# The last layer's down product as rows, with the activations stationary, in a two-layer hybrid decoder

## The chip, the cores and the metric

The kernel runs on one core of a Trainium2 chip. The metric is the device time in microseconds of one execution. Five engines work side by side: TensorE (PE, with its weight loads shown apart as PEld), VectorE (DVE), ScalarE (ACT), GpSimd (POOL) and SyncE (SP, which issues most DMAs).

## The reference

256 tokens with 2048 features go through two layers, each a token mixer and a dense SwiGLU feed-forward network (FFN), and a last RMS norm. All is float32. Layer 0 mixes by a convolution module, layer 1 by gated linear attention.

```python
D_MODEL = 2048; SEQ = 256; D_FF = 5632
def rms_norm(x, g):
    return x * lax.rsqrt(jnp.mean(x * x, axis=-1, keepdims=True) + EPS) * g

def swiglu_ffn(h, w_gate_up, w_down):
    a, g = jnp.split(h @ w_gate_up, 2, axis=-1)
    return (jax.nn.silu(a) * g) @ w_down

for i in range(DEPTH):
    h = mixer_i(rms_norm(x, norm_mix_g[i]))
    x = x + h
    x = x + swiglu_ffn(rms_norm(x, norm_ffn_g[i]), ffn_w_gate_up[i], ffn_w_down[i])
return rms_norm(x, final_norm_g)
```

## The kernel before

**Layout.** The residual stream lies in SBUF as `res`, features on the 128 partitions and the 256 tokens along the row: 16 tiles of 128 features, `res[:, 4g:4g+4, :]` being group g of 512 features. Products stay nearly float32 by a split: each operand is a high part (a rounded copy, made by ACT) and a low part (the remainder, by DVE), and hi\*hi + hi\*lo + lo\*hi are summed in PSUM.

**Weights.** SP streams all matrices in chunks of 1 MB (512 input features by 512 output features, as four k-tiles `kt`) through a ring of four buffers `raw`. For each chunk ACT writes `w_hi` (L496), DVE writes `w_lo` (L785), PE multiplies and signals `w_used`. SP loads a chunk once the remainder of the chunk four places before is made; ACT turns a chunk to `w_hi` once PE is done with the chunk four places before. All engines run in program order, so the order of the code is the order of the work.

**The wide form.** For all products but two, PE holds weights stationary (128 by 128) and moves activations. `wide_chunk` issues for each of 4 k-tiles and 4 output tiles a pair: 512 moving columns against `w_hi` (tokens of the high part and of the low part together, L1291), 256 against `w_lo` (L1293). That is 32 matmuls and 32 weight loads a chunk. The halves land in different columns of a bank, so DVE adds two tensors to the residual per group, `from_hi` (L1006) and `from_lo` (L1014).

**The FFN** runs in three parts (`PARTS`) of 4, 4 and 3 pairs: each pair makes 512 hidden features (8 gate/up chunks), then the part's hidden features go through `w_down`: 4 output groups of 4 (or 3) chunks, added to `res`. A group uses four of the eight PSUM banks (slot s = g % 2), and PE may start group g once DVE has read group g - 2 (`acc_read`).

**The row form.** The attention values (L1623) and the last output group of the last layer (`half_chunk`, L1685) are made the other way: activations stationary (128 tokens), 512 weight columns moving, so the result has tokens on partitions. A chunk is, for each token half a, 4 k-tiles by 3 matmuls of 512 columns (hi\*hi, hi\*lo, lo\*hi): 24 matmuls and 24 weight loads.

**The end.** In the last part of layer 1, ACT squares each finished group (L530) and multiplies it by the gain (L535), DVE reduces the squares over the features (L804 to L810). While PE makes the last group as rows, it turns `res` of that group into PSUM (`half_residual`, L1676), transposes the other three groups (`output_rows`, L1670) and sums the squares over partitions (L1701). When a token half is done (`half_out`), ACT squares the last group with a sum (L766), takes the root (L770), DVE inverts it, both scale the four groups of rows into `out_rows` (L775, L1247, L1250), and SP stores two pieces of 512 KB. The second half's tail ends the kernel.

## Time and profile before

| | |
|---|---|
| timed runs | 2193.17, 2194.74, 2196.64 us; median 2194.74 us |
| span of the profiled execution | 2192.3 us, first to last instruction |
| PE / PEld busy | 2177.5 us (99%) / 1922.3 us (88%) |
| DVE busy | 1405.7 us (64%) |
| ACT busy | 991.0 us (45%) |
| DMA | 400.46 MB, mean 183 GB/s |

The profile is one execution, whose own time is its span of 2192.3 us; the median of the timed runs is 2.4 us longer, for what lies around the span and for the spread of the runs. PE's busy time overlaps with itself, since matmuls are pipelined: what a matmul costs is read from start to start, not from its duration. A "wait" in these views is the idle time of an engine before an instruction, put down to what came last.

### The profile page before, as it was taken

How to read it: one execution, taken by the hardware profiler on the slowest of the kernel's cores; microseconds unless marked ns; L12 is line 12 of the kernel's file. 1: busy time of each engine (PE TensorE's matmuls, PEld its weight loads, DVE VectorE, ACT ScalarE, POOL GpSimd, SP SyncE). 2: the span in 40 equal slices, each digit the busy share in tenths (PEclk: the TensorE clock that was granted, in tenths of full speed). 3: DMA queues.
4: the chain of work that ended last, by engine and by line, in shares of the span. 5: the costliest groups of instructions: out<-in, count | busy, mean ns of one | idle time of the engine just before them, and what ended most of it. 6: DMA issues, size and time to landing. Idle time of an engine off the chain costs nothing.

```text
span 2192.3 us, 32460 instructions
## 1 busy us (share of the span) xinstructions
PE 2177.5 (99%) x12992; PEld 1922.3 (88%) x12992; DVE 1405.7 (64%) x1314; ACT 991.0 (45%) x821; POOL 203.2 (9%) x107
## 2 busy tenths in 40 slices
PE   8999999999999999999999999999999999999998
PEld 8999888888888888888888888888888888888887
DVE  7999785555555655556667777675555555555655
ACT  6666554443344433444363444554443344433444
POOL 7998000000000000000000000000000000000000
PEclk9999999999999999999999999999999999999999
DMA  9664456555555555655544435655555555555552
GB/s 248 182 186 158 152 191 214 188 195 191 187 175 198 174 205 179 210 173 192 192 154 154 150 120 192 209 175 199 185 191 192 189 194 179 198 188 187 174 209 77
DMA packets 250043, 400.46 MB, mean 183 GB/s; under 512 B 6407, under 2 KB 72143, under 8 KB 249935
## 3 DMA queue, kind: packets, MB, share of 16 engines
q1 hardware_dynamic: 249406, 398.74, 54.7%
q8 instruction: 57, 0.93, 0.2%
q0 software_dynamic: 352, 0.56, 0.1%
q14 instruction: 20, 0.16, 0.0%
q10 hardware_dynamic: 208, 0.07, 0.0%
HBM read 397.24 MB, written 2.10 MB: 182 GB/s over the span
## 4 chain that ended last, share of the span: by engine, by line
PE 92%; DVE 4%; issue 2%; DVEq 1%; DMA 0%; ACT 0%; SPq 0%; ACTq 0%
PE bank L1291 55%; PE bank L1293 27%; PE bank L1623 4%; DVE bank L942 2%; PE bank L1378 1%; PE bank L1608 1%; PE bank L1685 1%; PE bank L1365 1%; DMA raw<-in_conv_w_in 0%; DVEq L920 0%; PE bank L1393 0%; PE bank L1368 0%; DVE bank L936 0%; DVE bank L923 0%; PE bank L1397 0%
## 5 line engine op out<-in xcount | busy, mean ns | idle before, releaser
L1291 PE MATMUL bank<-x_both,w_hi 128*128 128x512 f32 x3328 | 1156.7, 394 | 0.0
L785 DVE TENSOR_TENSOR w_lo<-raw,w_hi 128x2048 fp32r<-128x2048 f32 x343 | 779.2, 2290 | 527.1 <-ACT w_hi L496 526.9
L496 ACT ACTIVATE w_hi<-raw 128x2048 fp32r<-128x2048 f32 x374 | 707.4, 1909 | 627.7 <-PE bank L1293 599.2
L1293 PE MATMUL bank<-x_both,w_lo 128*128 128x256 f32 x3328 | 922.6, 277 | 0.0
L1291 PEld LDWEIGHTS bank<-x_both,w_hi 128*128 128x128 f32 x3328 | 624.8, 188 | 145.8 <-issue 0.8
L1291 PE MATMUL bank<-h_both,w_hi 128*128 128x512 f32 x1872 | 649.4, 394 | 0.4 <-DVE h_both L986 0.4
L1293 PEld LDWEIGHTS bank<-x_both,w_lo 128*128 128x128 f32 x3328 | 625.5, 188 | 0.1
L1293 PE MATMUL bank<-h_both,w_lo 128*128 128x256 f32 x1872 | 518.5, 277 | 0.0
L1291 PEld LDWEIGHTS bank<-h_both,w_hi 128*128 128x128 f32 x1872 | 351.0, 187 | 82.0 <-issue 0.5
L1293 PEld LDWEIGHTS bank<-h_both,w_lo 128*128 128x128 f32 x1872 | 351.4, 188 | 0.0
L1378 PE MATMUL bank<-x_both,w_hi 128*128 128x256 f32 x832 | 150.0, 283 | 0.0
L376 POOL TENSOR_TENSOR w_lo<-raw,w_hi 128x2048 fp32r<-128x2048 f32 x31 | 143.5, 4633 | 5.6 <-DVE w_lo L785 5.6
L942 DVE SCALAR_TENSOR_TENSOR bank<-u,dw,bank 128x256 f32<-128x256 f32 x334 | 137.9, 485 | 0.0
L1378 PEld LDWEIGHTS bank<-x_both,w_hi 128*128 128x128 f32 x832 | 129.8, 192 | 0.1
L1378 PE MATMUL bank<-x_both,w_lo 128*128 128x256 f32 x416 | 117.7, 283 | 0.0
L485 POOL DMA_DIRECT2D last_gain<-in_final_norm_g x1 | 0.6, 597 | 1115.3 <-PE bank L1293 1115.3
L1623 PE MATMUL bank<-w_hi,x_both 128*128 128x512 f32 x256 | 81.2, 393 | 0.0
L1378 PEld LDWEIGHTS bank<-x_both,w_lo 128*128 128x128 f32 x416 | 79.9, 192 | 0.0
L476 POOL DMA_DIRECT2D gate_w<-in_gla_gate_w x1 | 1.2, 1226 | 631.2 <-PE bank L1293 631.2
L1054 DVE TENSOR_TENSOR tmp<-bank,act 128x1024 f32<-128x1024 f32 x22 | 27.0, 1225 | 49.6 <-ACT act L660 49.6
L665 ACT ACTIVATE act<-bank 128x1024 f32<-128x1024 f32 x22 | 22.6, 1027 | 79.7 <-PE bank L1293 79.7
L660 ACT ACTIVATE act<-bank 128x1024 f32<-128x1024 f32 x22 | 22.6, 1027 | 77.0 <-PE bank L1293 77.0
(227 smaller groups left out, 1232.2 us busy)
## 6 DMA issues: line engine op xcount, KB each, us to landing
raw<-in_ffn_w_gate_up SPq DMA_DIRECT2D x176, 1024.0 KB, 5.1
raw<-in_ffn_w_down SPq DMA_DIRECT2D x88, 1024.0 KB, 5.1
raw<-in_gla_w_in SPq DMA_DIRECT2D x48, 1024.0 KB, 5.3
raw<-in_conv_w_in SPq DMA_DIRECT2D x32, 1024.0 KB, 6.0
raw<-in_conv_w_out SPq DMA_DIRECT2D x16, 1024.0 KB, 5.1
raw<-in_gla_w_out SPq DMA_DIRECT2D x16, 1024.0 KB, 6.9
x_rows<-in_x SPq DMA_DIRECT2D x4, 512.0 KB, 6.4
out<-out_rows SPq DMA_DIRECT2D x4, 512.0 KB, 3.1
```

The source lines that it names most:

```text
L376: nc.gpsimd.tensor_tensor(w_lo[k][:, :, :], raw[k][:, :, :], w_hi[k][:, :, :].bitcast(F32), ALU.subtract).then_inc(lo_done, 1)
L496: nc.scalar.activation(w_hi[k][:, :, :], raw[k][:, :, :], ACT.Copy).then_inc(hi_done, 1)
L660: nc.scalar.activation(part_lo[0], from_lo[0], ACT.Copy).then_inc(lo_kept[0], 1)
L665: nc.scalar.activation(part_lo[1], from_lo[1], ACT.Copy).then_inc(lo_kept[1], 1)
L785: nc.vector.tensor_tensor(w_lo[k][:, :, :], raw[k][:, :, :], w_hi[k][:, :, :].bitcast(F32), ALU.subtract).then_inc(lo_done, 1)
L942: nc.vector.scalar_tensor_tensor(out=to, in0=tap, scalar=w, in1=acc, op0=ALU.mult, op1=ALU.add).then_inc(tap_done, 1)
L1054: nc.vector.tensor_tensor(tmp[0][:, :, :], from_hi[0], part_lo[0], ALU.add).then_inc(acc_read[0], 1)
L1291: mm(to, w_hi[k][:, kt, cols], xx[:, :, k0 + kt, :], start=(first and kt == 0), stop=False, skip_group_check=True)
L1293: ins = mm(to[:, 0:T], w_lo[k][:, kt, cols], xx[:, 0, k0 + kt, :], start=False, stop=(last and kt == 3), skip_group_check=True)
L1365: mm(to, conv_view(w_hi[k])[:, kt, :], xx[:, kt, :], start=(kt == 0 and j == 0), stop=False)
L1378: ins = mm(slot[t][:, 2 - 2 * h, :], conv_view(w[k])[:, kt, :], xx[:, kt, :], start=(kt == 0 and j == 0), stop=(kt == KT - 1 and j == 2))
L1623: ins = mm(rows_[:, a, :], xx[:, 4 * j + kt, tok], w[j][:, kt, :], start=(j == 0 and kt == 0 and i == 0), stop=(j == 3 and kt == 3 and i = ...
```

## The change

The whole down product of layer 1 is made in the row form, in all three parts and all four groups. For that the residual has to be rows too: in the first part PE transposes it, 8 transposes of 128 by 128 a group (`res_bank`, the two spare banks of the slot), before the group's products, and ACT copies it back in place (`res_rows`). DVE then adds one tensor a group (`row_group`). In the last part ACT squares each group with a sum along the row (`row_squares`), DVE multiplies by the gain (`gain_rows`), and no transposes, no reductions over features and no sums by PE are left in the last group: PE adds the residual of the last group by one product with the identity per token half. The loads of the gain over all partitions grow from 256 KB to 1 MB. The final scaling works in place in `out_rows`. The loops over groups of the first two parts are written out.

The core of the diff (semaphores and removed counterparts are cut):

```diff
-        last_gain = sb("last_gain", [P, GW], 32 * K)
-        last_scratch = sb("last_scratch", [P, GW], 34 * K)
+        last_gain = sb("last_gain", [P, D], 32 * K)
+        last_scratch = sb("last_scratch", [P, 4, GW], 40 * K)
...
+        rows_bank = [bank[:, 4 * s:4 * s + 2, :] for s in range(2)]
+        res_bank = [bank[:, 4 * s + 2:4 * s + 4, :] for s in range(2)]
+        res_rows = [res[:, 4 * g:4 * g + 4, :].rearrange("p (a k) t -> p a (k t)", a=2) for g in range(4)]
...
             pool.wait_ge(w_used, C_END - 12)
-            pool.dma_start(last_gain[:, :], final_norm_g.rearrange("(a d) -> a d", a=1)[:, 3 * GW:].broadcast_to([P, GW])
+            pool.dma_start(last_gain[:, :], final_norm_g.rearrange("(a d) -> a d", a=1).broadcast_to([P, D])
...
+            def row_squares(use0, g):
+
+                scalar.wait_ge(acc_read[g % 2], (use0 + g) // 2 + 1)
+                for a in range(2):
+                    ins = nc.scalar.activation(squared_rows[g][:, a, :], res_rows[g][:, a, :], ACT.Square,
+                                               accum_out=sq_part[:, 3 * a + g:3 * a + g + 1])
+                ins.then_inc(rows_sq, 1)
...
+                    if l == 1 and pt == 0:
+                        for g in range(4):
+                            hi_group(d0 + 4 * g, 2)
+                            scalar.wait_ge(res_t, g + 1)
+                            nc.scalar.activation(res_rows[g], res_bank[g % 2], ACT.Copy).then_inc(res_turned, 1)
+                            hi_group(d0 + 4 * g + 2, 2)
...
-                for g in range(2):
-                    scalar.wait_ge(half_rows[a], g + 1)
-                    nc.scalar.activation(out_rows[:, a, g * GW:(g + 1) * GW], rows_bank[a][g], ACT.Copy,
-                                         scale=rstd_tok[:, a:a + 1]).then_inc(rows_act[a], 1)
+                nc.scalar.activation(out_rows[:, a, 0:2 * GW], out_rows[:, a, 0:2 * GW], ACT.Copy,
+                                     scale=rstd_tok[:, a:a + 1]).then_inc(rows_act[a], 1)
...
+            def row_group(c_end, g, first):
+
+                dve.wait_ge(w_used, c_end + 1)
+                if first:
+                    dve.wait_ge(res_turned, g + 1)
+                nc.vector.tensor_tensor(res_rows[g], rows_bank[g % 2], res_rows[g], ALU.add).then_inc(acc_read[g % 2], 1)
...
+            def rows_and_gains(c0, chunks, use0):
+
+                for g in range(3):
+                    lo_group(c0 + chunks * g, chunks)
+                    row_group(c0 + chunks * (g + 1) - 1, g, False)
+                    if g == 1:
+                        dve.wait_ge(gain_in, 16)
+                    if g >= 1:
+                        gain_rows(use0, g - 1)
+                gain_rows(use0, 2)
...
+            def row_chunk(c, g, j, a, chunks, started=False):
+
+                k, tok = c % RING, slice(a * P, (a + 1) * P)
+                for kt in range(4):
+                    for n, (hh, w) in enumerate(((h_hi, w_hi), (h_hi, w_lo), (h_lo, w_hi))):
+                        ins = mm(rows_bank[g % 2][:, a, :], hh[:, 4 * j + kt, tok], w[k][:, kt, :],
+                                 start=(not started and j == 0 and kt == 0 and n == 0),
+                                 stop=(j == chunks - 1 and kt == 3 and n == 2), skip_group_check=True)
+                return ins
+
+            def rows_product(c0, u0, h0, chunks, first):
+
+                for g in range(4 if chunks == RING else 3):
+                    free_slot(g % 2, (u0 + g) // 2)
+                    if first:
+                        for a in range(2):
+                            for b in range(4):
+                                ins = nc.tensor.transpose(res_bank[g % 2][:, a, b * P:(b + 1) * P],
+                                                          res[:, 4 * g + b, a * P:(a + 1) * P], ident[:, :])
+                        ins.then_inc(res_t, 1)
+                    for j in range(chunks):
...
-            half_residual(0)
-            half_chunk(0, 0)
-            output_rows(0, 0)
...
             for a in range(2):
...
+                mm(rows_bank[1][:, a, :], ident[:, :], res_rows[3][:, a, :], start=True, stop=False, skip_group_check=True)
+                for j in range(3):
+                    c = C_END - 3 + j
+                    pe.wait_ge(lo_done, c + 1)
+                    ins = row_chunk(c, 3, j, a, 3, started=True)
+                ins.then_inc(half_out, 1)
```

PE, before, where the first part's gate/up chunks end and its first down chunk begins (names: `h_both` the hidden features, `w_hi`, `w_lo` the weights; the moving operand stands first):

```order
L1501 UNCONDITIONAL_BRANCH
L1501 ISA
L1302 ISA [waits acc_read0]
L1291 MATMUL bank<-h_both,w_hi_57 128x512 [waits hid_ready,lo_done]
L1293 MATMUL bank<-h_both,w_lo_61 128x256
L1291 MATMUL bank<-h_both,w_hi_57 128x512
L1293 MATMUL bank<-h_both,w_lo_61 128x256
```

PE, of the change, at the same place:

```order
L1583 MATMUL bank<-ident,res 128x128 [waits acc_read0]
L1583 MATMUL bank<-ident,res 128x128 x7
L1571 MATMUL bank<-w_hi_57,h_both 128x512 [waits hid_ready,lo_done]
L1571 MATMUL bank<-w_lo_61,h_both 128x512
L1571 MATMUL bank<-w_hi_57,h_both 128x512 x2
L1571 MATMUL bank<-w_lo_61,h_both 128x512
```

Eight transposes now stand ahead of the products of each of the first part's four groups, pairs of 512 and 256 columns have become triples of 512, and the waits are the same ones.

PE, before, around the last output group's first chunk:

```order
L1676 MATMUL bank<-ident,res 128x128 [waits acc_read1]
L1676 MATMUL bank<-ident,res 128x128 x3
L1685 MATMUL bank<-w_hi_58,h_both 128x512 [waits lo_done]
L1685 MATMUL bank<-w_lo_62,h_both 128x512
...
L1670 MATMUL bank<-ident,act 128x128 [waits xn_done]
L1670 MATMUL bank<-ident,act 128x128 x3
L1685 MATMUL bank<-w_hi_59,h_both 128x512 [waits lo_done]
```

PE, of the change, at the same place:

```order
L1756 MATMUL bank<-res,ident 128x512 [waits acc_read1]
L1571 MATMUL bank<-w_hi_58,h_both 128x512 [waits lo_done]
L1571 MATMUL bank<-w_lo_62,h_both 128x512
...
L1571 MATMUL bank<-w_hi_58,h_both 128x512
L1571 MATMUL bank<-w_hi_59,h_both 128x512 [waits lo_done]
```

The products of the last group now follow one another with no transposes between them; the six blocks of four transposes (L1670) and the sums (L1701) are gone, and one matmul of 512 columns a token half takes the place of four of 128.

DVE, of the change, in the last part, from the second group's last remainder on:

```order
L1044 TENSOR_TENSOR res<-bank,res 128x1024 [waits w_used]
L1050 TENSOR_TENSOR out_rows<-res,last_gain 128x2x512 [waits acc_read0,gain_in]
L808 TENSOR_TENSOR w_lo_62<-raw_54,w_hi_58 128x2048 [waits hi_done]
L808 TENSOR_TENSOR w_lo_63<-raw_55,w_hi_59 128x2048 [waits hi_done]
L808 TENSOR_TENSOR w_lo_64<-raw_56,w_hi_60 128x2048 [waits hi_done]
```

The wait for the gain (`gain_in`) stood at the end of the program before, behind the last remainders; now it stands ahead of the last three.

## Rows read from the trace of the kernel before

**Rows 1.** The page: span, busy time, and PE's busy share and granted clock in slices
```profile
span 2192.3 us, 32460 instructions
PE 2177.5 (99%) x12992; PEld 1922.3 (88%) x12992; DVE 1405.7 (64%) x1314; ACT 991.0 (45%) x821; POOL 203.2 (9%) x107
PEclk9999999999999999999999999999999999999999
```

**Rows 2.** The page: shares of the chain that ended last
```profile
PE 92%; DVE 4%; issue 2%; DVEq 1%; DMA 0%; ACT 0%; SPq 0%; ACTq 0%
```

**Rows 3.** Waits of ACT from 2100 to 2170 us: total, times, longest
```profile
ACT w_hi L496 <- PE bank L1293: 14.0, 5, 3.6
```

**Rows 4.** Timeline of ACT, layer 1: start us, duration us, in brackets the idle time before
```profile
1910.31 1.92 ACT L496 ACTIVATE w_hi<-raw 128x2048 fp32r<-128x2048 f32 x1 [3.63 <-PE bank L1293]
...
1971.33 1.92 ACT L496 ACTIVATE w_hi<-raw 128x2048 fp32r<-128x2048 f32 x1 [3.63 <-PE bank L1293]
```

**Rows 5.** Timeline of ACT, attention values, one whole row chunk without other PE work
```profile
1237.96 1.93 ACT L496 ACTIVATE w_hi<-raw 128x2048 fp32r<-128x2048 f32 x1 [1.25 <-PE bank L1623]
1243.40 1.91 ACT L496 ACTIVATE w_hi<-raw 128x2048 fp32r<-128x2048 f32 x1 [3.51 <-PE bank L1623]
```

**Rows 6.** Timeline of PE, last output group
```profile
2169.56 0.40 PE L1685 MATMUL bank<-w_lo,h_both 128*128 128x512 f32 x1
...
2171.87 0.39 PE L1685 MATMUL bank<-w_hi,h_both 128*128 128x512 f32 x1
...
2176.99 0.48 PE L1685 MATMUL bank<-w_hi,h_both 128*128 128x512 f32 x1
2177.31 0.39 PE L1685 MATMUL bank<-w_lo,h_both 128*128 128x512 f32 x1
...
2185.04 0.39 PE L1685 MATMUL bank<-w_hi,h_both 128*128 128x512 f32 x1
```

**Rows 7.** Timeline of PE, start of the kernel: eight transposes and what follows
```profile
10.58 1.04 PE L1329 MATMUL bank<-ident,x_rows 128*128 128x128 f32 x8
11.45 0.28 PE L1319 MATMUL bank<-ident 128*128 128x128 f32 x1
```

**Rows 8.** The chain that ended last, from 2165 us: start us, us, what
```profile
2165.42 0.89 PE bank L1676 x8
2166.31 2.74 PE bank L1685 x12
2169.05 0.44 PE bank L1670 x4
...
2176.24 1.00 PE bank L1676 x8
2177.24 8.21 PE bank L1685 x36
```

**Rows 9.** Timeline: last gate/up chunk's copy, one remainder, one group squared
```profile
2115.54 1.03 ACT L665 ACTIVATE act<-bank 128x1024 f32<-128x1024 f32 x1 [3.63 <-PE bank L1293]
...
2145.28 2.29 DVE L785 TENSOR_TENSOR w_lo<-raw,w_hi 128x2048 fp32r<-128x2048 f32 x1 [1.60 <-ACT w_hi L496]
...
2151.34 1.06 ACT L530 ACTIVATE tmp<-res 128x1024 f32<-128x1024 f32 x1 [6.09 <-DVE res L1014]
```

**Rows 10.** Timeline, the end: ACT's and DVE's last work, SP's last issues
```profile
2186.72 1.27 ACT L775 ACTIVATE out_rows<-bank,rstd_tok 128x512 f32<-128x512 f32 x2 [0.23 <-DVE rstd_tok L1245]
...
2187.38 0.74 DVE L1250 TENSOR_SCALAR out_rows<-bank,rstd_tok 128x512 f32<-128x512 f32 x1
2188.01 0.81 SPq L366 DMA_DIRECT2D out<-out_rows  x2
```

**Rows 11.** Windows 1090.66 to 1094.00 and 2165.26 to 2176.10: engines' busy time, then PEclk, DMA share, GB/s
```profile
1090.66:1094.00 3.34, 3.34 (x11) 2.86 (x11) 3.34 (x8) 0.00 (x0) 0.00 (x0) 0.50 0.38 81
2165.26:2176.10 10.84, 10.84 (x63) 9.19 (x61) 7.29 (x6) 3.26 (x7) 0.00 (x0) 1.00 0.01 2
```

**Rows 12.** DMA issues from 2105 us on: KB each, median us to landing
```profile
last_gain<-in_final_norm_g POOLq DMA_DIRECT2D x1, 256.0 KB, 4.3
```

More of the change, by code:

```diff
@@ L260, in trunk @@
         half_out = sem("half_out")
-        half_rows = [sem(f"half_rows{a}") for a in range(2)]
+        res_t = sem("res_t")
+        res_turned = sem("res_turned")
+        rows_sq = sem("rows_sq")
+        rows_gain = sem("rows_gain")
+        rows_total = sem("rows_total")
         half_sq = sem("half_sq_done")
-        bias_stat = sem("bias_stat")
         bias_done = sem("bias_done")
@@ L363, in _ @@
                 for n, rows in enumerate((rows_act, rows_vec)):
-                    sp.wait_ge(rows[a], 2)
+                    sp.wait_ge(rows[a], n + 1)
                     cols = slice(2 * n * GW, (2 * n + 2) * GW)
@@ L681, in ffn @@
                             gain(g)
-                            if l == 0 and g == 0:
+                            if g == 0:
                                 scalar.wait_ge(gate_in, 48)
@@ L1014, in residual_group, with gain_rows @@
                 nc.vector.tensor_tensor(to, from_lo[s], to, ALU.add).then_inc(acc_read[s], 1)
+            def row_group(c_end, g, first):
[3 more added lines that the diff above has]
+                nc.vector.tensor_tensor(res_rows[g], rows_bank[g % 2], res_rows[g], ALU.add).then_inc(acc_read[g % 2], 1)
+            def gain_rows(use0, g):
+                dve.wait_ge(acc_read[g % 2], (use0 + g) // 2 + 1)
+                cols = slice(g * GW, (g + 1) * GW)
+                nc.vector.tensor_tensor(out_rows[:, :, cols], res_rows[g], over(last_gain[:, cols], 2),
+                                        ALU.mult).then_inc(rows_gain, 1)
+            def rows_and_gains(c0, chunks, use0):
+                for g in range(3):
+                    lo_group(c0 + chunks * g, chunks)
[5 more added lines that the diff above has]
+                gain_rows(use0, 2)
             def residual_and_squares(c0, n_group, n0, gains, chunks=4):
@@ L1075, in ffn @@
                     d0 = c0 + 8 * pairs
-                    if pt < 2:
+                    if l == 1 and pt < 2:
+                        for g in range(4):
+                            lo_group(d0 + 4 * g)
+                            row_group(d0 + 4 * g + 3, g, pt == 0)
+                    elif l == 1:
+                        rows_and_gains(d0, pairs, u0 + 2 * pairs)
+                    elif pt < 2:
                         with dve.Fori(0, 2) as i:
@@ L1664, in _ @@
             ffn(1, 4 * KT, 16, 8)
-            def output_rows(g, a):
-                pe.wait_ge(xn_done, 2 * KT + 4 * g + 4)
-                for b in range(4):
-                    ins = nc.tensor.transpose(rows_bank[a][g][:, b * P:(b + 1) * P], act[:, 4 * g + b, a * P:(a + 1) * P],
-                                              ident[:, :])
-                ins.then_inc(half_rows[a], 1)
-            def half_residual(a):
-                for b in range(4):
-                    mm(rows_bank[a][3][:, b * P:(b + 1) * P], res[:, 12 + b, a * P:(a + 1) * P], ident[:, :],
-                       start=(b == 0), stop=False, skip_group_check=True)
@@ L1679, in half_chunk @@
-            def half_chunk(a, j):
-                c = C_END - 3 + j
-                pe.wait_ge(lo_done, c + 1)
-                k, tok = c % RING, slice(a * P, (a + 1) * P)
-                for kt in range(4):
-                    for n, (hh, w) in enumerate(((h_hi, w_hi), (h_hi, w_lo), (h_lo, w_hi))):
-                        ins = mm(rows_bank[a][3], hh[:, 4 * j + kt, tok], w[k][:, kt, :], start=False,
-                                 stop=(j == 2 and kt == 3 and n == 2), skip_group_check=True)
-                if j == 2:
-                    ins.then_inc(half_out, 1)
```

59 lines of the change are left out of this document (30 added, 29 removed).

## The prediction

> **What bounds the kernel now.** I read the page first: PE is busy 99% of a span of 2192.3 us, at the full clock in every slice [rows 1]. The chain that ended last is PE for 92% [rows 2]. Then the waits in the stage that changes: ACT, which prepares the weights, idles up to 3.6 us at a time until PE has freed a buffer [rows 3]. So ACT, DVE (behind ACT) and the DMAs (behind DVE) are ahead of PE, and PE is ahead of nobody: a microsecond more or less on PE in this stage is a microsecond of the kernel, and one on another engine is nothing so long as it stays under these 3.6 us a chunk. Only behind PE's last product do ACT, DVE and the stores set the end.
>
> **What a chunk costs, before.** PE's rows overlap, so I take the pace from ACT, which starts on a new buffer each time PE ends a chunk: 12 starts from 1910.31 to 1971.33 us, so 11 chunks of the wide form in 61.02 us, **5.547 us a chunk** [rows 4]. This stretch lies in the second part's down product.
>
> **What a chunk costs as rows.** The kernel has this form in two places. In the last group, from 2177.31 to 2185.04 us, 34 steps of one matmul take 7.73 us: 0.2274 us each, 5.457 us for 24 [rows 6]. Among the attention values one chunk with nothing between takes 5.44 us [rows 5]. The dearest stretch is 2169.56 to 2171.87 us, 10 steps in 2.31 us, so 0.2310 us and 5.544 us a chunk [rows 6]; DVE and ACT are at work there, in the first half of the group. Columns do not explain a gain: both forms move 12,288 columns a chunk. The difference is 24 matmuls in place of 32. Moving 512 columns at 2.4 GHz is 0.2133 us, so 0.014 us comes on top of each matmul; a wide pair is 5.547/16 = 0.3467 us against 0.3200 us of columns, 0.0133 us a matmul again. Eight fewer are 0.107 us. I take the 5.457 us of the longest stretch, a saving of 0.092 us a chunk, since this stretch has company from ACT or DVE for a part of it only, as a chunk has.
>
> The Trainium skill (TensorE: Matmul & The Clock Gate, Back-to-back issue gap) gives an isolated matmul its columns at the clock plus 2.5 ns. By that rule eight matmuls fewer are 0.02 us, the 41 chunks give 0.8 us, and the sum would come out near 2195.4 us, no gain. The trace disagrees, with its 13 ns a matmul in a stream that has a weight load ahead of each [rows 4, 6].
>
> **The terms.**
> 1. Chunks that change form: 4 groups of 4 chunks in each of two parts, 3 groups of 3 in the last, 41. 41 x 0.092 = **3.8 us less**. Ends: 41 x 0.107 = 4.4 (a chunk of 5.44) and 41 x 0.003 = 0.1 (the dearest stretch).
> 2. Transposes of the residual, 8 in each of 4 groups, on PE, where nothing hides them. Eight in a row at the start of the kernel take 11.45 - 10.58 = 0.87 us [rows 7]. In the last group four cost 0.44 us of the chain [rows 8], and that holds a slower first step of the product behind them: 2176.99 to 2177.31 is 0.32 us against 0.23, 0.09 more [rows 6]. So eight are between 2 x 0.44 - 0.09 = 0.79 and 0.87 + 0.09 = 0.96 us. I take 0.88, **3.5 us more**; ends 3.2 and 3.8. Below nothing is excluded: PE is busy before and behind, and the instructions are added.
> 3. The last group. Before, PE's chain from 2165.42 to 2185.45 us is 20.03 us [rows 8]. It holds two residual products (0.89 and 1.00), 72 matmuls of rows, three blocks of transposes at 0.44, and the sums. What is left is residual plus 36 matmuls, twice: 2 x (0.89 + 8.21) = 18.2 us, **1.8 us less**. The residual product's 512 columns are now one matmul, not four of 128; I give it the price of the four, since the columns are the same. Ends: 0.79 to 1.00 for it and 8.16 to 8.32 for the rows, so 2.1 and 1.4.
> 4. Behind the last product, square, root and inverse are the same. ACT's scaling was two copies of 512 from PSUM, 1.27 us [rows 10], and becomes one of 1024 in SBUF; the nearest row is 1.06 us [rows 9]. SP issues both last stores at 2188.01, right behind ACT [rows 10], so **0.2 us less**. DVE's last product (0.74 us) now reads SBUF, not PSUM; the rows have no such form at this size. If it were twice as fast, the second store could follow sooner: 0.5 us at best, 0 at worst. The 12 transposes that stood behind the last product ran beside ACT and cost nothing before.
>
> Costed at nothing: ACT's four copies of the turned residual, about 1.06 us each by the same size [rows 9], in the 3.6 us that it idles in every chunk [rows 3, 4]. They stand behind the wait `res_t`, and the next `w_hi` is queued behind them, for which DVE and then PE wait; but ACT comes to it after a `w_hi` that itself waits for the group's first chunk, so the transposes have long been done. Without that cover it would be 4 us. DVE does one add a group in place of two, and one gain product in place of a reduction and an add: less work. The squares by rows come where ACT's squares and gains stood, and the gains leave ACT. The bias needs DVE's add, ACT's squares and three small operations behind the third group, and is asked for half a group later, 0.89 + 8.21 = 9.1 us [rows 8].
>
> Sum: -3.8 + 3.5 - 1.8 - 0.2 = -2.3 us, against the profiled span 2192.3 - 2.3 = 2190.0 us. The median of the timed runs is 2.4 us above that span, so 2194.7 - 2.3 = **2192.4 us**. This is 0.11%; a measurement of this kernel tells about 0.2%, or 4.4 us, from no change. The best ends together: -4.4 + 3.2 - 2.1 - 0.5 = -3.8, 2190.9 us. The worst: -0.1 + 3.8 - 1.4 = +2.3, 2197.0 us.
>
> **The rivals.**
> - *The row form is no cheaper.* With ACT and DVE at work beside it, as in most of each chunk, rows go at the 5.54 us of the dearest stretch. Then -0.1 + 3.5 - 1.8 - 0.2 = +1.4, **2196.1 us**. For it: that stretch is the one with most work beside it. Against it: the chunk of 5.44 us among the attention values has a whole `w_hi` beside it as well [rows 5]. The Trainium skill's rule above comes out between this and the forecast, and speaks for it.
> - *The clock falls behind the transposes*, and the kernel is **slower**. At 1090.66 us the granted clock is 0.50, the 1.2 GHz level, for 3.3 us [rows 11], after a block of small products of the attention gate. In these 3.34 us PE starts 11 matmuls, some 5.3 pairs, which take 5.3 x 0.347 = 1.8 us at 2.4 GHz, so a fall costs 1.5 us. Behind each of the four blocks of transposes it would be 6 us: 2192.4 + 6.0 = **2198.4 us**; it decides from two falls on (3 us against the 2.3 won). Against it: the last group has three blocks of four transposes, the sums and a residual product within 10.8 us at clock 1.00 [rows 11]. The Trainium skill (TensorE: Matmul & The Clock Gate, Part 4: PE-mode transpose) states that the full clock does not engage for transposes; the rows here show none that lost it.
> - *The gain comes late*, slower too. It grows from 256 KB in 4.3 us [rows 12] to 1 MB, 17 us in proportion, and its wait now stands ahead of the last three remainders on DVE. It is issued when the last gate/up chunk ends, at 2115.5 us [rows 9]; PE needs the first of those remainders at 2165.4 [rows 8], and one takes 2.3 us [rows 9]. DVE can wait until 2163, 47 us after the issue. Past that each microsecond is one of the kernel. It would need three times the proportional time.
> - *Clearly faster*: best ends for all terms and something more, such as transposes half hidden behind the weight loads. Under 2190.3 us.
>
> **How the numbers follow.** Forecast (2190.9 to 2194.5) 0.58; rows no cheaper (2194.5 to 2197.0) 0.18; the clock 0.07, half of it over 4.4 us slower; the gain or another new wait 0.04, slower; clearly faster 0.13. So faster by over 0.2%: 0.13, with 0.02 of the forecast that spread between runs carries over, 0.15; slower by over 0.2%: 0.035 + 0.04, with a little of the rest 0.09; within it 0.76. The range takes in both sums of ends: low 2190.3, a little under the best, high 2197.0.
>
> **What would show it.** In the profile of after: ACT's starts on `w_hi` in the down stages 5.44 to 5.47 us apart (5.54: the first rival). PE's matmuls fewer by 41 x 8 = 328 before what the rest adds. From a group's first transpose to its first row matmul 0.8 us, and the next step 0.3. From the last group's first instruction to `half_out` 18.2 us. PEclk 1.00 in the first down stage; DVE not idle for `last_gain`. The prediction is wrong if PE idles anywhere in the written-out groups, or if the chunk pace is outside 5.44 to 5.54 us.

## The result: the change is 3.35 us slower, 0.16%

| | median of the runs, us | lowest to highest | runs |
|---|---|---|---|
| before | 2195.54 | 2193.0 to 2197.6 | 18 |
| with the change | 2198.89 | 2196.42 to 2202.1 | 18 |

The ratio is 1.0016, with a 95% interval of 1.001 to 1.0022. The forecast was 2192.4 us, range 2190.3 to 2197.0: it has the wrong sign and misses by 6.5 us, of which 0.8 us is the median of before, which came out higher over 18 runs than over the first 3.

The page of the change: span, busy time and PE's granted clock, which answer to [rows 1]. PE's share of the chain that ended last is 92% as before.

```profile
span 2197.6 us, 31653 instructions
PE 2182.4 (99%) x12656; PEld 1918.8 (87%) x12656; DVE 1388.6 (63%) x1302; ACT 991.1 (45%) x820; POOL 203.1 (9%) x107
PEclk9999999999999999999999999999999999999999
```

PE makes 336 matmuls fewer and is busy 5 us longer, at the same clock. So no other engine became the bound: something on PE got dearer. The place is found by laying the same program point of both kernels side by side: the start of the ACT instruction that PE's last matmul of a chunk releases.

| program point | before, us | change, us | change is behind by |
|---|---|---|---|
| first w_hi behind the convolution's mixing | 228.43 | 229.52 | 1.09 |
| layer 0's FFN, first copy (L660, now L674) | 334.19 | 337.20 | 3.01 |
| a query/key copy (L693, now L717) | 1098.11 | 1100.01 | 1.90 |
| layer 1's FFN, part one's gate/up ends | 1627.43 | 1629.35 | 1.92 |
| part one's down product ends | 1716.18 | 1720.09 | 3.91 |
| part two's gate/up ends | 1893.67 | 1900.98 | 7.31 |
| part two's down product ends | 1982.42 | 1988.09 | 5.67 |
| part three's gate/up ends | 2115.54 | 2123.76 | 8.22 |
| PE's last product ends | 2185.47 | 2190.84 | 5.37 |

(1982.42 is the last start of [rows 4] plus two chunks.) Up to 1627 us the two kernels run the same instructions on PE, and their difference there comes and goes: more on it below. From there on the change loses 1.99, 3.40 and 2.55 us and wins 1.64 and 2.85. The down products do what was forecast. The two losses of 3.40 and 2.55 us, 5.95 us together, are in the **gate/up products of parts two and three, which the change doesn't touch**.

Timeline of ACT in the change, from the last row chunks of part one into part two's gate/up (start us, duration us, in brackets the idle time before):

```profile
1714.71 1.92 ACT L502 ACTIVATE w_hi<-raw 128x2048 fp32r<-128x2048 f32 x1 [3.52 <-PE bank L1571]
1720.09 1.92 ACT L502 ACTIVATE w_hi<-raw 128x2048 fp32r<-128x2048 f32 x1 [3.46 <-PE bank L1571]
1725.73 1.93 ACT L502 ACTIVATE w_hi<-raw 128x2048 fp32r<-128x2048 f32 x1 [3.72 <-PE bank L1349]
1731.38 1.92 ACT L502 ACTIVATE w_hi<-raw 128x2048 fp32r<-128x2048 f32 x1 [3.72 <-PE bank L1349]
...
1742.69 1.03 ACT L674 ACTIVATE act<-bank 128x1024 f32<-128x1024 f32 x1 [3.73 <-PE bank L1349]
```

The same chunks before:

```profile
1721.73 1.92 ACT L496 ACTIVATE w_hi<-raw 128x2048 fp32r<-128x2048 f32 x1 [3.63 <-PE bank L1293]
1727.27 1.92 ACT L496 ACTIVATE w_hi<-raw 128x2048 fp32r<-128x2048 f32 x1 [3.63 <-PE bank L1293]
...
1738.37 1.03 ACT L660 ACTIVATE act<-bank 128x1024 f32<-128x1024 f32 x1 [3.63 <-PE bank L1293]
```

A wide chunk takes 5.65 us behind the row form where it takes 5.55 us before, the same 32 matmuls, with ACT waiting for PE in both (3.73 and 3.63 us: the wait shows the pace). It goes on for all 32 and 24 chunks: (7.31 - 3.91) / 32 = 0.106 us each. PE starts nothing late and doesn't idle; each pair is longer. Timeline of PE in the change, three pairs (they start 0.36 and 0.35 us apart, 0.353 over the whole chunk of 16):

```profile
1721.64 0.40 PE L1347 MATMUL bank<-x_both,w_hi 128*128 128x512 f32 x1
1721.88 0.28 PE L1349 MATMUL bank<-x_both,w_lo 128*128 128x256 f32 x1
1722.00 0.40 PE L1347 MATMUL bank<-x_both,w_hi 128*128 128x512 f32 x1
1722.24 0.28 PE L1349 MATMUL bank<-x_both,w_lo 128*128 128x256 f32 x1
1722.35 0.40 PE L1347 MATMUL bank<-x_both,w_hi 128*128 128x512 f32 x1
```

and before (0.35 and 0.35 us apart, 0.3467 over the chunk [rows 4]):

```profile
1721.87 0.40 PE L1291 MATMUL bank<-x_both,w_hi 128*128 128x512 f32 x1
1722.10 0.28 PE L1293 MATMUL bank<-x_both,w_lo 128*128 128x256 f32 x1
1722.22 0.39 PE L1291 MATMUL bank<-x_both,w_hi 128*128 128x512 f32 x1
...
1722.57 0.40 PE L1291 MATMUL bank<-x_both,w_hi 128*128 128x512 f32 x1
```

It isn't the clock. Windows of the change: the first down part with its transposes, and the gate/up of part two (us, busy time and count by engine, then PEclk, DMA share, GB/s; PEclk is the last figure but two):

```profile
1623.50:1720.00 96.50, 96.50 (x451) 80.53 (x450) 47.35 (x24) 38.08 (x23) 0.00 (x0) 1.00 0.55 186
1720.00:1901.00 181.00, 181.00 (x1026) 156.90 (x1025) 99.29 (x54) 74.44 (x47) 0.00 (x0) 1.00 0.55 186
```

### The profile page after: what moved, and what is told of

Read it like the earlier page. It is cut to its first block, busy times and chain, and to the rows that moved or that the text cites. A ratio compares the mean times of both kernels' runs of the same rounds, so it can differ in the third digit from the quotient of the medians.

```text
span 2197.6 us, 31653 instructions
## 1 busy us (share of the span) xinstructions
PE 2182.4 (99%) x12656; PEld 1918.8 (87%) x12656; DVE 1388.6 (63%) x1302; ACT 991.1 (45%) x820; POOL 203.1 (9%) x107
## 4 chain that ended last, share of the span: by engine, by line
PE 92%; DVE 4%; issue 2%; DVEq 1%; DMA 0%; ACT 0%; SPq 0%; ACTq 0%
PE bank L1347 48%; PE bank L1349 24%; PE bank L1571 11%; PE bank L1710 4%; DVE bank L965 2%; PE bank L1434 1%; PE bank L1695 1%; PE bank L1421 1%; DVEq L943 0%; PE bank L1449 0%; PE bank L1424 0%; DMA x_rows<-in_x 0%; DVE bank L959 0%; PE bank L1453 0%; DVE bank L946 0%
## 5 line engine op out<-in xcount | busy, mean ns | idle before, releaser
L1347 PE MATMUL bank<-h_both,w_hi 128*128 128x512 f32 x1216 | 423.6, 393 | 0.4 <-DVE h_both L1009 0.4
L1349 PE MATMUL bank<-h_both,w_lo 128*128 128x256 f32 x1216 | 340.0, 280 | 0.0
L1347 PEld LDWEIGHTS bank<-h_both,w_hi 128*128 128x128 f32 x1216 | 227.8, 187 | 52.4 <-issue 0.5
L1349 PEld LDWEIGHTS bank<-h_both,w_lo 128*128 128x128 f32 x1216 | 229.7, 189 | 0.0
L1571 PE MATMUL bank<-w_hi,h_both 128*128 128x512 f32 x704 | 219.5, 391 | 0.0
L1571 PEld LDWEIGHTS bank<-w_hi,h_both 128*128 128x128 f32 x704 | 132.2, 188 | 27.8 <-issue 0.5
L1571 PE MATMUL bank<-w_lo,h_both 128*128 128x512 f32 x352 | 137.0, 389 | 0.0
L1571 PEld LDWEIGHTS bank<-w_lo,h_both 128*128 128x128 f32 x352 | 66.1, 188 | 14.0 <-issue 0.5
```

Of the source, the lines that this page charges most:

```text
L1347: mm(to, w_hi[k][:, kt, cols], xx[:, :, k0 + kt, :], start=(first and kt == 0), stop=False, skip_group_check=True)
L1349: ins = mm(to[:, 0:T], w_lo[k][:, kt, cols], xx[:, 0, k0 + kt, :], start=False, stop=(last and kt == 3), skip_group_check=True)
L1571: ins = mm(rows_bank[g % 2][:, a, :], hh[:, 4 * j + kt, tok], w[k][:, kt, :], start=(not started and j == 0 and kt == 0 and n == 0), stop= ...
```

## The experiments

The two theories at the start: **(A)** the wide form has two paces, and PE keeps through a stretch the one in which it entered it; entered from rows that is the longer. **(B)** the place of the code, or something else that the change moved, makes these loops longer.

### Is it there without the change, and every time?

Both kernels again, unchanged.

> The kernel before, unchanged, profiled once more. In its first profile all wide stages went at 5.55 us a chunk; in the first profile of the change the output product of the convolution (228 to 331 us), of the same code in both, went at 5.65. If the pace is drawn anew in each execution (theory A: two paces, set by how a stage is entered), this profile may show 5.65 in some wide stage. If the pace is fixed by where the code lies (theory B), it shows 5.55 everywhere, as the first did.

> The change, unchanged, profiled once more. Theory A: the gate/up products behind the rows of the first two parts again at 5.65 us a chunk, since they are entered in the same way each time, while the stages at 228 us and 1064 us may differ from the first profile. Theory B: every stage exactly as in the first profile, those at 228 and 1064 us at 5.65 too.

The change took 2201.85 us, its gate/up chunks in parts two and three 5.65 us again. The kernel before took 2197.53 us, with all chunks of the last layer's FFN at 5.55 us. But in this execution of it the long pace stood elsewhere, in the convolution's output product and in both stretches of query/key chunks. For the first of these places, timeline of ACT, the kernel before run again, then its first profile:

```profile
228.61 1.92 ACT L496 ACTIVATE w_hi<-raw 128x2048 fp32r<-128x2048 f32 x1 [3.67 <-PE bank L1293]
...
256.88 1.91 ACT L496 ACTIVATE w_hi<-raw 128x2048 fp32r<-128x2048 f32 x1 [1.64 <-PE bank L1293]
```

```profile
228.43 1.92 ACT L496 ACTIVATE w_hi<-raw 128x2048 fp32r<-128x2048 f32 x1 [3.57 <-PE bank L1293]
...
256.16 1.92 ACT L496 ACTIVATE w_hi<-raw 128x2048 fp32r<-128x2048 f32 x1 [1.09 <-PE bank L1293]
```

And the first stretch of query/key chunks, the kernel before run again:

```profile
1078.41 1.91 ACT L496 ACTIVATE w_hi<-raw 128x2048 fp32r<-128x2048 f32 x1 [2.89 <-PE bank L1293]
1084.06 1.92 ACT L496 ACTIVATE w_hi<-raw 128x2048 fp32r<-128x2048 f32 x1 [3.73 <-PE bank L1293]
```

Five chunks lie between the two starts in the convolution: 28.27 us in the one and 27.73 us in the other, 5.65 and 5.55 each again, in one and the same program. The long pace isn't a thing of the change, then, and theory B as it was put (the first profile again, stage by stage) fails here already. This explains most of the differences ahead of 1627 us in the table too: the change's profile had the long pace in that stage (+1.92 us of the 3.01). One such stage is a good part of the 4.6 us between the shortest and the longest run of before.

### Break the stream behind the rows, or ahead of them

A product of one column with the identity (plain float32; PE shows two instructions for it) goes between the row blocks of parts one and two and the next gate/up loop. As the control, the same products stand ahead of the row blocks: same number, nearly the same places in the code.

```diff
+                    if l == 1 and pt > 0:          # behind the rows
+                        free_slot(0, u0 // 2)
+                        mm(bank[:, 0, 0:1], ident[:, :], ident[:, 0:1], start=True, stop=True, skip_group_check=True)
```

```diff
+                    if g == 0 and chunks == RING:  # control: ahead of the rows
+                        mm(bank[:, 0, 0:1], ident[:, :], ident[:, 0:1], start=True, stop=True, skip_group_check=True)
```

> The change with one float32 product of one column (two matmul instructions) behind the rows of parts one and two, ahead of the gate/up loop. Theory A (the slow pace comes from running straight from rows into the wide form): gate/up of parts two and three back to 5.55 us a chunk, 56 x 0.107 = 6.0 us less and 0.3 us more for the two products, so some 5.7 us under the change: 2193.2 us, under the kernel before by 2. Theory B (place of the code): the loop moves by two instructions only, and the time stays within 1 us of the change, or moves in both this run and the next.

> The control: the same two products at the other end of the row blocks, ahead of them, so that the code behind is moved by just as much, but the gate/up loop is entered from rows as in the change. Theory A: gate/up stays at 5.65 us a chunk, 2199 us. Theory B: the same time as the run with the product behind the rows.

| | us | ratio to before (2195.66) | gate/up chunk |
|---|---|---|---|
| product behind the rows | 2193.85 | 0.9992 (0.9983 to 1.0001) | 5.55 |
| product ahead of the rows | 2198.39 | 1.0016 (1.0006 to 1.0025) | 5.65 |

Timeline of ACT with the product behind the rows:

```profile
1719.09 1.92 ACT L502 ACTIVATE w_hi<-raw 128x2048 fp32r<-128x2048 f32 x1 [3.46 <-PE bank L1571]
1724.86 1.92 ACT L502 ACTIVATE w_hi<-raw 128x2048 fp32r<-128x2048 f32 x1 [3.86 <-PE bank L1349]
1730.41 1.92 ACT L502 ACTIVATE w_hi<-raw 128x2048 fp32r<-128x2048 f32 x1 [3.63 <-PE bank L1349]
```

One chunk of 5.77 us pays for the product, and the rest go at 5.55. Two products of one column take 4.5 us off the kernel against their twins ahead of the rows. Theory A stands so far, and the place of the code falls as the cause.

### What kind of product breaks it

Three other products at the same place behind the rows: 128 and 512 columns of the rounded type (fp32r) that the kernel's own products have, and, later, 128 columns of float32.

```diff
+                        mm(bank[:, 0, 0:P], h_hi[:, 0, 0:P], h_hi[:, 0, 0:P], start=True, stop=True, skip_group_check=True)  # short
```
```diff
+                        mm(bank[:, 0, :], h_hi[:, 0, 0:P], h_hi[:, 0:2, :], start=True, stop=True, skip_group_check=True)  # row
```
```diff
+                        mm(bank[:, 0, 0:P], ident[:, :], ident[:, :], start=True, stop=True, skip_group_check=True)  # float32
```

> As the run with the small product behind the rows, but the product is of the split type, 128 columns against 128 (one matmul instruction, no float32). If what matters is that a short instruction breaks the even beat of the rows, gate/up goes at 5.55 us a chunk. If it takes a float32 product, it stays at 5.65. The rhythm theory says 5.55, without much certainty.

> Control for any product at that place: one of the split type with 512 columns, which goes on in the beat of the rows. The rhythm theory: gate/up stays at 5.65 us a chunk. If any added product helps, whatever its length, 5.55.

> The change with a float32 product of 128 columns behind the rows (one column restored the fast pace, a split product of 128 columns did not). 5.55 in gate/up if it takes a float32 product; 5.65 if it takes a very short one.

One run of each: 2197.2, 2198.74 and 2191.54 us. With either fp32r product the chunks stay at 5.65 us, against my expectation for the short one; with the float32 product they are 5.55. The start that tells them apart, ACT with 128 columns of fp32r and then of float32:

```profile
1729.14 1.92 ACT L502 ACTIVATE w_hi<-raw 128x2048 fp32r<-128x2048 f32 x1 [3.73 <-PE bank L1349]
1734.80 1.92 ACT L502 ACTIVATE w_hi<-raw 128x2048 fp32r<-128x2048 f32 x1 [3.74 <-PE bank L1349]
```
```profile
1728.90 1.92 ACT L502 ACTIVATE w_hi<-raw 128x2048 fp32r<-128x2048 f32 x1 [3.63 <-PE bank L1349]
1734.45 1.92 ACT L502 ACTIVATE w_hi<-raw 128x2048 fp32r<-128x2048 f32 x1 [3.63 <-PE bank L1349]
```

So not any interruption does it, and with float32 1 and 128 columns both do. Of the products tried here only the plain float32 ones work. What in them does it isn't told apart: a float32 product is two matmuls and two weight loads in PE's trace, each fp32r product was one, and two fp32r products in a row were not tried.

### Does such a product always give the short pace?

The products behind the rows, with two more in the convolution's output product and one each ahead of query/key groups 2 and 3; the last four alone in the kernel before; and one small product ahead of the gate/up loops in the kernel before, where no rows stand. (The first of the two in the convolution adds a column of zeros to a bank in use.)

```diff
+                    if j == 2 and s == 0:
+                        pe.wait_ge(zero_set, 1)
+                        mm(bank[:, 0, 0:1], ident[:, :], zero[:, :], start=False, stop=False, skip_group_check=True)
...
+                if s == 0:
+                    mm(bank[:, 0, 0:1], ident[:, :], ident[:, 0:1], start=True, stop=True, skip_group_check=True)
...
+                if g in (1, 2):
+                    mm(bank[:, 4 * (g % 2), 0:1], ident[:, :], ident[:, 0:1], start=True, stop=True, skip_group_check=True)
```

> The change with the small products behind the rows, and four more: in the middle and in the second half of the convolution's output product (228 to 331 us), and ahead of the second and the third query/key group (1070 to 1142 us), the places where profiles of all kernels have shown now 5.55 and now 5.65 us a chunk. Theory: those stages at 5.55 in every run, some 1.0 us less on average at the first place and 0.7 at the second, 0.8 more for four products, so 2193 us and a narrower spread. Rival (the pace there is not set by the entry): 2194.6 us and the spread as before.

> The kernel before with the same four products in the convolution's output and the query/key groups, and no rows. By the theory 2194.8 us against 2195.7; then the run with all products against this one is the worth of the row form by itself, which the terms of the prediction put at 2.3 us less.

> The kernel before, all wide, with the small float32 product ahead of the gate/up loops of parts two and three of the last layer. In the runs with products at the query/key groups, the product stood behind a wide matmul of 256 columns and the stage went to 5.65 us a chunk. If the pace is set by how the beat is entered, and has nothing to do with rows as such, gate/up and down of part two (48 chunks) go at 5.65 here: 5 us slower, 2200 to 2201 us, and up to 8.7 us if the second product leaves it slow. If it is the rows that slow what follows, this kernel is 0.4 us slower than before, no more.

| | us | ratio to before |
|---|---|---|
| change, all products | 2194.31 | 0.9996 (0.9987 to 1.0005) |
| before, the four products | 2196.27 | 1.0004 (0.9995 to 1.0013) |
| before, a product ahead of gate/up | 2195.53 | 1.0002 (0.9992 to 1.0011) |

No. The first two came out 1.3 and 1.5 us over what was expected, and the runs spread as widely as before. Gate/up was at 5.55 us where rows stood ahead, and stayed at 5.55 us in the kernel before, where I had expected the product to bring the long pace. But both stretches of query/key groups were at the long pace behind their product, in both kernels (4 of 4). Timeline of ACT, the change with all products:

```profile
1077.14 1.92 ACT L505 ACTIVATE w_hi<-raw 128x2048 fp32r<-128x2048 f32 x1 [3.10 <-PE bank L1352]
1082.79 1.92 ACT L505 ACTIVATE w_hi<-raw 128x2048 fp32r<-128x2048 f32 x1 [3.73 <-PE bank L1352]
```

In the 13 other profiles with paired chunks, where no product stands there, the first of these stretches was long in 4 and the second in 8, the kernel before among both kinds. So a float32 product is no switch to the short pace. That it brings the long one here is likely from 4 of 4, and not shown. The two kernels with the four products differ by the change and its products behind the rows alone: 2196.27 - 2194.31 = 2.0 us in favour of the row form, with intervals (each about 2 us to either side) that overlap.

### Other ways out: order in a pair, the convolution's stage, rows in the last part only

```diff
+                        if lo_first:   # gate/up of parts two and three: 256 columns first
+                            mm(to[:, 0:T], w_lo[k][:, kt, cols], xx[:, 0, k0 + kt, :], start=(first and kt == 0), stop=False,
+                               skip_group_check=True)
+                            ins = mm(to, w_hi[k][:, kt, cols], xx[:, :, k0 + kt, :], start=False,
+                                     stop=(last and kt == 3), skip_group_check=True)
+                            continue
```

> The change, with the pairs of the gate/up loops of parts two and three in the other order: 256 columns against the low part first, then 512 against the high part. No product is added. If the entry sets the beat, the stage may fall into the fast one (5.55, some 6 us less than the change: 2193 us) or stay; it costs nothing. If the slow pace belongs to the code behind the rows, 2199 us.

It took 2198.71 us, ratio 1.0018 (1.0009 to 1.0028), with chunks of 5.65 us: turning the pair round changes nothing that these runs can tell.

The next has the products behind the rows and the two in the convolution's output product (the first two pieces of the diff of the section before).

> The products behind the rows, and the two in the convolution's output product, without those at the query/key groups that made things slower. 0.45 us more for the two, 1.0 less on average for the stage at 228 us: 2193.3 us, against 2193.85 with the products behind the rows alone, and no run over 2195.

2193.47 us, ratio 0.9997 (0.9988 to 1.0006), and two of the 11 runs over the 2195 us that none was to pass. Gate/up 5.55 us; but five chunks of the convolution's output product, with one product among them, took 28.17 and then 28.49 us in this profile, against 27.96 us both times in the two kernels with all four products. So the products there don't hold off the long pace, and this is the kernel with the products behind the rows once more.

Rows in the last part alone, with 24 transposes there (and the last group's residual as before), parts one and two wide:

```diff
-                    if l == 0:
+                    if l == 0 or pt < 2:
                         residual_product(c0 + 8 * pairs, u0 + 2 * pairs, (hid_ready, h0), True, pairs)
                     else:
-                        rows_product(c0 + 8 * pairs, u0 + 2 * pairs, h0, pairs, pt == 0)
+                        rows_product(c0 + 8 * pairs, u0 + 2 * pairs, h0, pairs, True)
```

> A part of the change alone: rows only in the last part, where the residual of three groups is turned; parts one and two wide as before, so no wide product follows rows in this layer. By the terms: 9 chunks 1.0 us less, 24 transposes with their slower first step 2.8 more, last group 1.8 less: level with before, 2195.6 us. If the slowdown of the change came from anything in the last part, it would show here.

2194.93 us, ratio 1.0 (0.9991 to 1.0009), as expected. No gate/up stands behind rows, and all of it is at 5.55 us. From the last gate/up chunk's end to the end of PE's last product this profile has 2184.85 - 2115.00 = 69.85 us, the kernel before 2185.47 - 2115.54 = 69.93 us; the terms say 1.0 less, 2.8 more and 1.9 less. So neither the row form in the last part nor the new end costs anything that was not in the sum.

### A stream that has one pace

If the pairs are the trouble, a chunk whose matmuls are ordered otherwise may have no second pace: for each k-tile the four products of 512 columns, then the four of 256, in every wide chunk, with the change and without.

```diff
                     for nb in range(4):
-                        cols = slice(nb * P, nb * P + P)
-                        to = bank[:, 4 * s + nb, :]
-                        mm(to, w_hi[k][:, kt, cols], xx[:, :, k0 + kt, :], start=(first and kt == 0), stop=False,
-                           skip_group_check=True)
-                        ins = mm(to[:, 0:T], w_lo[k][:, kt, cols], xx[:, 0, k0 + kt, :], start=False,
-                                 stop=(last and kt == 3), skip_group_check=True)
+                        mm(bank[:, 4 * s + nb, :], w_hi[k][:, kt, nb * P:nb * P + P], xx[:, :, k0 + kt, :],
+                           start=(first and kt == 0), stop=False, skip_group_check=True)
+                    for nb in range(4):
+                        ins = mm(bank[:, 4 * s + nb, 0:T], w_lo[k][:, kt, nb * P:nb * P + P], xx[:, 0, k0 + kt, :],
+                                 start=False, stop=(last and kt == 3), skip_group_check=True)
```

> The change, with every wide chunk of the whole kernel in another order: per k-tile the four products of 512 columns first, then the four of 256, in place of alternating pairs. Same instructions, same columns. If the slow pace is a beat of the alternating pairs, no stage goes at 5.65 us, and the wide chunks go at 5.55 whatever precedes them: 6 us less than the change, and 1 to 2 less for the stages at 228 and 1100 us, so 2191 to 2193 us, with the spread of the runs narrower. If the slow pace does not need the alternation, gate/up behind the rows stays at 5.65: 2199 us.

> The kernel before in the same order, so that the pair tells the worth of the row form with no slow stage in either. By the terms of the prediction as measured since (chunks -4.4, turns +3.7, last group -1.9) the change is 2.6 us faster than this kernel. This kernel itself: 1 to 2 us less than before, 2193.5 to 2194.5 us; the same as before if the order does not matter.

With the change 2210.12 us (ratio 1.0067, 1.0053 to 1.0081), without 2215.81 us (1.0091, 1.0077 to 1.0105). Timeline of ACT in the first, behind the rows (row chunks up to 1733.12, then wide ones):

```profile
1727.74 1.92 ACT L502 ACTIVATE w_hi<-raw 128x2048 fp32r<-128x2048 f32 x1 [3.52 <-PE bank L1570]
...
1738.70 1.92 ACT L502 ACTIVATE w_hi<-raw 128x2048 fp32r<-128x2048 f32 x1 [3.67 <-PE bank L1348]
1744.32 1.92 ACT L502 ACTIVATE w_hi<-raw 128x2048 fp32r<-128x2048 f32 x1 [3.70 <-PE bank L1348]
1749.93 1.92 ACT L502 ACTIVATE w_hi<-raw 128x2048 fp32r<-128x2048 f32 x1 [3.70 <-PE bank L1348]
```

The wide chunks of both kernels, behind rows or not, now go at 5.61 to 5.62 us (the first behind the rows at 5.58). The guess that they would go at 5.55 us was wrong, and both kernels are 11 to 20 us slower than they are with pairs. That is no good as a kernel, but a good balance: with one pace only, the change is **5.7 us faster**, and none of the five runs of one overlaps with the five of the other. By the prediction's own terms it should be: 41 chunks x (5.615 - 5.44) = 7.2 less, 3.7 more for the transposes, 1.9 and 0.1 less for the last group and the tail, 5.5 us.

## Why the prediction was wrong

**The step that failed** is a term that the sum hasn't got. That in this stage a microsecond on PE is one of the kernel was right, but the sum held only the chunks and products that the change rewrites. The "5.547 us a chunk" was read from one stretch of one execution and taken as a property of the wide form, and so the 56 wide gate/up chunks behind the rows stood in the sum at nothing, without a reason given. They measured 56 x 0.106 = 5.95 us more. No rival had it either, since all of them asked what the new instructions cost or make wait. Nor did the list of what would show the prediction wrong: the row chunks came out at 5.44 us, PE is busy through all 563.30 us from 1627.50 to 2190.80, and the sign was wrong all the same, because no line of that list looked at code that the change leaves as it is.

The terms themselves, from the table of program points and the profile of the change:

| term | forecast, us | measured, us | from |
|---|---|---|---|
| 1. 41 chunks as rows | -3.8 | -4.4 | 41 x (5.547 - 5.44) |
| 2. 32 transposes | +3.5 | +3.7 | 4 x 0.92 |
| 3. last group | -1.8 | -1.9 | 20.03 to 18.13 |
| 4. tail | -0.2 | -0.1 | 6.83 to 6.76 |
| wide chunks behind rows | 0 | +5.95 | 56 x 0.106 |
| sum | -2.3 | +3.3 | profiles from 1627 us on: 5.3 - 1.92 = 3.4 |

1. Row chunks take 5.44 us, the low end, with ACT and DVE at work beside them. Timeline of ACT in the change, 12 chunks in the 65.27 us between these two starts; it answers to [rows 4], and the rival of 5.54 us falls.

```profile
1917.37 1.92 ACT L502 ACTIVATE w_hi<-raw 128x2048 fp32r<-128x2048 f32 x1 [3.52 <-PE bank L1571]
...
1982.64 1.92 ACT L502 ACTIVATE w_hi<-raw 128x2048 fp32r<-128x2048 f32 x1 [3.52 <-PE bank L1571]
```

2. Transposes: 0.79 us to the first row matmul and 0.32 to the next (forecast 0.8 and 0.3). The chunk that begins a group ends 6.36 us behind the one before (1652.10 to 1658.46 in ACT's starts), 0.92 more than 5.44. Timeline of PE, to be held against [rows 7]:

```profile
1629.15 1.04 PE L1583 MATMUL bank<-ident,res 128*128 128x128 f32 x8
1629.94 0.47 PE L1571 MATMUL bank<-w_hi,h_both 128*128 128x512 f32 x1
1630.26 0.39 PE L1571 MATMUL bank<-w_lo,h_both 128*128 128x512 f32 x1
```

The clock stayed at 1.00 over all four blocks (window 1623.50 to 1720.00 above), so that rival falls, and with it, for blocks this short, the warning of the Trainium skill (TensorE: Matmul & The Clock Gate, Part 4: PE-mode transpose) that the full clock does not engage for transposes. (The rival's price of a fall counts 11 matmuls where PE starts 10 in those 3.34 us, 1.6 us in place of 1.5; the steps between profiles at the end of this text are 1.5.)

3. The last group, the chain that ended last in the change (start us, us, what); it answers to [rows 8]. 2190.82 - 2172.69 = 18.13 us, forecast 18.2.

```profile
2172.69 0.86 PE bank L1756 x2
2173.55 8.20 PE bank L1571 x36
2181.75 0.86 PE bank L1756 x2
2182.61 8.21 PE bank L1571 x36
2190.82 0.02 issue
```

4. The tail, against [rows 10]: ACT's one copy in SBUF is dearer than the 1.06 us taken (1.15), DVE's last product cheaper than 0.74.

```profile
2192.09 1.15 ACT L798 ACTIVATE out_rows<-out_rows,rstd_tok 128x1024 f32<-128x1024 f32 x1 [0.23 <-DVE rstd_tok L1302]
...
2192.76 0.48 DVE L1306 TENSOR_SCALAR out_rows<-out_rows,rstd_tok 128x512 f32<-128x512 f32 x1
2193.26 0.81 SPq L372 DMA_DIRECT2D out<-out_rows  x2
```

What was costed at nothing cost nothing: ACT's copies of the turned residual (1.00 us each) lie in its waits, and DVE never waits for the gain, whose 1 MB landed in 6.7 us, not in the 17 us of the proportion [rows 12]:

```profile
last_gain<-in_final_norm_g POOLq DMA_DIRECT2D x1, 1024.0 KB, 6.7
```

**The stretch that the change touches, by itself.** From the start of ACT's copy at the end of part one's gate/up (1627.43 us in the table of program points) to ACT's start behind PE's last product (2185.47 us), profiles of different executions agree within 0.02 us, and the stages whose pace or clock varied between executions lie ahead of it:

| kernel | profiles | stretch, us | against before |
|---|---|---|---|
| before, and with the four early products | 3 | 558.03 to 558.04 | |
| with the change | 2 | 561.49 | +3.45 |
| change, float32 product behind the rows | 4 | 555.96 to 555.98 | -2.07 |
| rows in the last part alone | 1 | 557.96 | -0.08 |
| four of 512 columns first, without and with the change | 1 each | 564.54, 559.16 | -5.38 between them |

The two ends of it with the change, then with the product of one column behind the rows (timeline of ACT):

```profile
1629.35 1.03 ACT L679 ACTIVATE act<-bank 128x1024 f32<-128x1024 f32 x1 [3.63 <-PE bank L1349]
...
2190.84 0.60 ACT L791 ACTIVATE tmp<-bank 128x512 f32<-128x512 f32 x1 [5.25 <-PE bank L1571]
```
```profile
1628.35 1.03 ACT L679 ACTIVATE act<-bank 128x1024 f32<-128x1024 f32 x1 [3.63 <-PE bank L1349]
...
2184.33 0.60 ACT L791 ACTIVATE tmp<-bank 128x512 f32<-128x512 f32 x1 [5.25 <-PE bank L1571]
```

The terms give +3.35, -2.2 (with 0.4 us back for the two products), -0.1 and -5.4 us for these, the tail left out. So these differences, small against the spread of whole runs, belong to this stretch and not to the earlier stages.

**What is shown and what isn't.** Shown: the loss lies in the wide chunks behind the rows (12 of 12 such stretches at 5.65 us, in the change twice, with the products ahead of the rows, with either fp32r product and with the pairs turned); a float32 product in between takes it away (8 of 8 stretches, in four kernels); it is neither the place of the code, the last part, nor the clock; and where the stream has one pace, the change wins what its terms add up to. Open: what in PE carries the two rhythms, whether it is the type of the float32 product or its two instructions that counts, why it gives the short pace behind rows but not ahead of the query/key groups, and what draws the pace of the stages that change it from execution to execution.

**The better kernel.** With one small float32 product behind the rows of parts one and two the change takes 2193.85 us, and in its second form 2193.47 us, 1.8 and 1.9 us under the median of before measured with each. The ratios are 0.9992 and 0.9997, and both intervals include 1, so by the whole time a gain isn't shown. In the stretch above it is, 2.07 us in four profiles of four, near what the terms gave (2.7 us less, with 0.4 us back for the two products). The float32 product of 128 columns gave 2191.54 us, in a single run.

## What to carry to other kernels

Where PE is the bound, the price of a form belongs to the stream that it stands in: when a change puts another form ahead of code that it doesn't touch, give that code a term in the sum, with the dearest pace that any profile shows for it. Read the pace stage by stage, from the starts of an engine that waits for PE, and in more than one execution of the same program: a single profile showed one of two paces as if it were the only one. And where a result contradicts the terms, lay the same program points of both kernels side by side before any mechanism is doubted; here that one table named the stage.

## What the runs showed that was not expected

- The same 32 matmuls of a wide chunk have two steady paces at the same granted clock of 1.00, 5.547 and 5.65 us (0.3467 and 0.353 us a pair of 512 and 256 columns), each kept through stretches of 24 and 32 chunks. With the four of 512 columns first they have one, 5.61 us; as triples of 512 columns 5.44 us for the same number of columns.
- In the profile before, the clock fell to 0.50 for 3.3 us behind the attention gate [rows 11]. In the change's it stayed at 1.00 over 1090 to 1100 us. The step from the last chunk there to the next copy (1087.18 to 1098.11 us before, 1090.61 to 1100.01 in the change) took 9.4 to 9.5 us in 7 of the 15 profiles of kernels with paired chunks, 10.9 to 11.0 in 5, 12.5 to 12.6 in 3: steps of 1.5 us, the price that the prediction gave a fall of the clock. The clock follows them where I looked: it stood at 0.50 for some 3.4 us with the product behind the rows (a step of 10.99 us), for some 6.8 us in the change's second profile (12.57), and at 1.00 throughout with rows in the last part alone (9.49). They too spread the runs.
- DVE's TENSOR_SCALAR of 128x512 float32 took 0.48 us from SBUF where it took 0.74 us from PSUM [rows 10].
